# Experts in eleven passes instead of twelve, with a third expert of fixed place

## What is computed

```python
glog = hf @ w_rg + b_rg                       # 4 groups
gsel = argmax(glog);  gw = softmax(glog)[gsel]
elog = (hf @ w_re + b_re)[group gsel]         # 4 experts of that group
top_v, top_i = top_k(elog, 2)
wts  = softmax(top_v) * gw
act  = silu(hf @ w_gate[e]) * (hf @ w_up[e]) * comb[e]   # 1024 -> 256
out  = sum over experts of act @ w_down[e]               # 256 -> 1024
```

## Time and profile before

| | |
|---|---|
| time, median of 3 runs | 797.34 us (795.62 to 798.36) |
| span of the profiled execution | 795.5 us |
| median of the runs less that span | 1.84 us |
| PE busy | 762.2 us, 96% |
| DMA bytes | 136.50 MB, mean 172 GB/s |
| passes | 12 (12 gathers of rows, 12 stores) |

### The profile page before, as it was taken

One profiled execution on the slowest core, in us unless ns is written; L12 is line 12 of the kernel. 1 busy time (PEld: TensorE's weight loads), 2 busy tenths in 40 slices (PEclk: granted clock), 3 DMA queues, 4 the chain that ended last, 5 costly groups with the idle time before them and its releaser, 6 DMA issues.

```text
span 795.5 us, 12983 instructions
## 1 busy us (share of the span) xinstructions
PE 762.2 (96%) x5070; PEld 494.9 (62%) x5070; DVE 379.9 (48%) x850; ACT 204.9 (26%) x485; POOL 106.8 (13%) x160
## 2 busy tenths in 40 slices
PE   8999999999999999889999999999999999998995
PEld 5455588777778788555566775445556564654442
DVE  3269523997232323766624378434732212214865
ACT  3011213112223354654523200134111111123223
POOL 3000006000000311334500100011111101015002
PEclk9999999999999999999999999999999999999998
DMA  9640493841440499200030279003799999996002
GB/s 324 160 126 0 112 278 139 99 133 57 140 97 17 139 233 266 94 1 1 1 120 2 96 216 384 1 14 128 282 407 409 416 418 416 417 373 211 17 14 106
DMA packets 81287, 136.50 MB, mean 172 GB/s; under 512 B 33926, under 2 KB 57546, under 8 KB 77010
## 3 DMA queue, kind: packets, MB, share of 16 engines
q1 hardware_dynamic: 64700, 110.17, 41.7%
q0 software_dynamic: 3728, 13.38, 4.9%
q10 hardware_dynamic: 12798, 12.12, 4.6%
HBM read 116.55 MB, written 21.19 MB: 173 GB/s over the span
## 4 chain that ended last, share of the span: by engine, by line
PE 80%; DMA 8%; DVE 6%; issue 2%; ACT 2%; POOL 1%; DVEq 0%; SPq 0%; POOLq 0%; ACTq 0%
PE ps L1215 29%; PE ps L1300 10%; PE ps L1656 6%; PE ps L1904 5%; PE ps L1788 4%; PE ps L1222 3%; PE ps L1776 3%; DMA merged<-in_w_exp_down 3%; DMA w_slot<-in_w_exp_down 2%; PE ps L1441 2%; PE ps L1820 2%; PE ps L1491 2%; PE ps L1537 2%; PE ps L1518 2%; DMA wgu<-expert_rows,pos_i 1%
## 5 line engine op out<-in xcount | busy, mean ns | idle before, releaser
L1215 PE MATMUL ps<-w_slot,hT 128*128 128x396 f32 (+1 forms) x192 | 71.1, 529 | 0.6 <-DMA w_slot<-in_w_in 0.4
L1215 PE MATMUL ps<-hT,w_slot 128*128 128x288 f32 x256 | 63.1, 407 | 0.0
L1215 PEld LDWEIGHTS ps<-hT,w_slot 128*128 128x128 f32 x256 | 48.3, 190 | 13.9 <-issue 0.8
L1215 PEld LDWEIGHTS ps<-w_slot,hT 128*128 128x128 f32 x192 | 36.1, 190 | 32.5 <-issue 13.4
L2987 DVE SCALAR_TENSOR_TENSOR th<-th,ps 128x256 f32<-128x256 f32 x12 | 5.1, 421 | 103.2 <-ACT th L2248 103.2
L1788 PE MATMUL ps<-w_slot,hT 128*32 128x256 f32 x544 | 49.7, 380 | 0.0
L1300 PE MATMUL ps<-hT,w_slot 128*128 128x288 f32 x144 | 37.3, 407 | 0.0
L1215 PE MATMUL ps<-qg,w_slot 128*128 128x288 f32 x128 | 33.7, 408 | 0.0
L1788 PEld LDWEIGHTS ps<-w_slot,hT 128*32 128x32 f32 x544 | 26.3, 110 | 10.0 <-issue 2.3
L2728 DVE TENSOR_REDUCE nm_p<-ps 128x2 f32<-128x256 f32 (+3 forms) x32 | 25.0, 819 | 15.6 <-PE ps L1491 15.5
L1300 PEld LDWEIGHTS ps<-hT,w_slot 128*128 128x128 f32 x144 | 27.3, 190 | 7.6 <-issue 0.2
(11 more groups left out here) (508 smaller groups left out, 1416.5 us busy)
## 6 DMA issues: line engine op xcount, KB each, us to landing
merged<-in_w_exp_down SPq DMA_DIRECT2D x10, 1024.0 KB, 15.9
w_slot<-in_w_in SPq DMA_DIRECT2D x8, 1024.0 KB, 7.7
wgu<-in_w_exp_gate SPq DMA_DIRECT2D x8, 1024.0 KB, 12.1
wgu<-in_w_exp_up SPq DMA_DIRECT2D x8, 1024.0 KB, 14.1
w_slot<-in_w_exp_gate SPq DMA_DIRECT2D x8, 1024.0 KB
w_slot<-in_w_exp_up SPq DMA_DIRECT2D x8, 1024.0 KB
w_slot<-in_w_exp_down SPq DMA_DIRECT2D x6, 1024.0 KB
expert_rows<-onsaT ACTq DMA_DIRECT2D x12, 512.0 KB, 8.2
```

The lines of the kernel that those rows point to most:

```text
L1215: ins = pe.matmul(out, a, b, start=(n == 0), stop=(n == len(pairs) - 1))
```

## The change

There are 11 passes. The first one holds 96 rows of expert 0 and 32 of expert 1, the second the other 64 of expert 1 and a column of 64. Expert 2 is the third expert of fixed place and has the third pass to itself with 128 places. The other columns are 128, 128, four of 96 and seven of 64. The columns' order of loading is new, and so is the order on SP's queue. The gate and up weights of expert 2 are loaded as set 3 behind the second down load, before the router's order is known; set 2 is loaded behind the wait for the first gather as before. The first pass is now computed by `gate_up_of_two`, and the lists of rows and places are put together accordingly (`rows_of_passes`, the tables of GpSimd, the first list on VectorE).

```diff
-RANK_OF_COLUMN = [0, 1, 6, 2, 7, 8, 3, 9, 10, 4, 14, 5, 11, 12, 13, 15]
-COLUMNS_OF_PASS = [[0], [1, 12], [2, 12], [3], [4, 13], [5, 13], [6], [7, 14], [8, 14], [9], [10, 15], [11]]
+RANK_OF_COLUMN = [0, 1, 2, 5, 6, 3, 7, 8, 9, 10, 4, 11, 12, 13, 14, 15]
+UNITS_OF_PASS = [[0, 0, 0, 1], [1, 1, 11, 11], [2] * 4, [3, 3, 3, 12], [4, 4, 4, 12], [5] * 4, [6, 6, 6, 13], [7, 7, 7, 13],
+                 [8, 8, 14, 14], [9, 9, 15, 15], [10] * 4]
...
-LOADED = [0, 1, 12, 2, 3, 4, 13, 5, 6, 7, 14, 8, 9, 10, 15, 11]
+LOADED = [0, 1, 11, 2, 3, 12, 4, 5, 6, 13, 7, 8, 14, 9, 15, 10]
...
             load_down(1, 1)
+            load_gate_up(3, 2)
             sp.wait_ge(order_made, 1)
-            at_column = {0: 0, 1: 1}
+            at_column = {0: 0, 1: 1, 2: 2}
...
             sp.wait_ge(hg_ld[0], 16)
-            for l in range(2, NX):
-                read_column(l)
-                load_gate_up(l, expert(l))
+            read_column(2)
+            load_gate_up(2, expert(2))
             load_down(2, expert(2))
...
                 gate_up_weights(5)
+                gate_up_weights(6)
                 down_weights(3)
-                gate_up_weights(6)
                 gate_up_weights(7)
                 down_weights(4)
+                down_weights(5)
                 gate_up_weights(8)
-                down_weights(5)
                 down_weights(6)
                 gate_up_weights(9)
+                gate_up_weights(10)
                 down_weights(7)
-                gate_up_weights(10)
                 gate_up_weights(11)
                 down_weights(8)
+                down_weights(9)
                 gate_up_weights(12)
-                down_weights(9)
                 down_weights(10)
                 gate_up_weights(13)
+                gate_up_weights(14)
                 down_weights(11)
-                gate_up_weights(14)
                 gate_up_weights(15)
                 down_weights(12)
                 down_weights(13)
...
                 pe.matmul(out[:, 0:NPASS], ident[:], by_column[:, 0:NPASS], start=True, stop=True)
+                pe.matmul(out[96:P, 0:1], ident[:, 0:32], by_column[:, 1:2], start=True, stop=True)
                 for h in range(2):
-                    pe.matmul(out[96:P, 1 + h:8 + h:3], ident[:, 32 * h:32 * h + 32], by_column[:, 12:15], start=True, stop=True)
-                return pe.matmul(out[64:P, 10:11], ident[:, 0:64], by_column[:, 15:16], start=True, stop=True)
+                    pe.matmul(out[96:P, 3 + h:7 + h:3], ident[:, 32 * h:32 * h + 32], by_column[:, 12:14], start=True, stop=True)
+                pe.matmul(out[0:64, 1:2], ident[:, 32:96], by_column[:, 1:2], start=True, stop=True)
+                pe.matmul(out[64:P, 1:2], ident[:, 0:64], by_column[:, 11:12], start=True, stop=True)
+                return pe.matmul(out[64:P, 8:10], ident[:, 0:64], by_column[:, 14:16], start=True, stop=True)
...
-                gate_up(j, 0, 0, lambda: turn_rows(j, 1, 1, 0))
+                gate_up_of_two(j, 0, 0, lambda: turn_rows(j, 1, 1, 0))
...
-            tt(idx[:, 0:1], first_f[:, 0:1], o[:, NE:NE + 1], ALU.add).then_inc(first_made, 1)
+            tt(idx[0:96, 0:1], first_f[0:96, 0:1], o[0:96, NE:NE + 1], ALU.add)
+            tt(idx[96:P, 0:1], first_f[0:32, 1:2], o[0:32, NE + 1:NE + 2], ALU.add).then_inc(first_made, 1)
```

More of the change, by code:

```diff
@@ L61 @@
 MAXR = -(-ROWS // CAP)
-RANK_OF_COLUMN = [0, 1, 6, 2, 7, 8, 3, 9, 10, 4, 14, 5, 11, 12, 13, 15]
-COLUMNS_OF_PASS = [[0], [1, 12], [2, 12], [3], [4, 13], [5, 13], [6], [7, 14], [8, 14], [9], [10, 15], [11]]
-NPASS = len(COLUMNS_OF_PASS)
+RANK_OF_COLUMN = [0, 1, 2, 5, 6, 3, 7, 8, 9, 10, 4, 11, 12, 13, 14, 15]
+UNITS_OF_PASS = [[0, 0, 0, 1], [1, 1, 11, 11], [2] * 4, [3, 3, 3, 12], [4, 4, 4, 12], [5] * 4, [6, 6, 6, 13], [7, 7, 7, 13],
+                 [8, 8, 14, 14], [9, 9, 15, 15], [10] * 4]
+NPASS = len(UNITS_OF_PASS)
 OF_PARITY = [-(-NPASS // 2), NPASS // 2]
-LOADED = [0, 1, 12, 2, 3, 4, 13, 5, 6, 7, 14, 8, 9, 10, 15, 11]
-LAST_PASS = [max(n for n, columns in enumerate(COLUMNS_OF_PASS) if column in columns) for column in LOADED]
+LOADED = [0, 1, 11, 2, 3, 12, 4, 5, 6, 13, 7, 8, 14, 9, 15, 10]
+LAST_PASS = [max(n for n, columns in enumerate(UNITS_OF_PASS) if column in columns) for column in LOADED]
 NX = 4
@@ L73, in unit_loads @@
 def unit_loads(n):
-    loads = [LOADED.index(column) for column in COLUMNS_OF_PASS[n]]
-    own = 2 if COLUMNS_OF_PASS[n][-1] == NE - 1 else 3
-    return [loads[0]] * own + [loads[-1]] * (4 - own)
+    return [LOADED.index(column) for column in UNITS_OF_PASS[n]]
 def down_before(l):
@@ L1101, in row_of @@
                 pool.iota(out, [[step, out.shape[-1]]], base=first, channel_multiplier=0, allow_small_or_imprecise_dtypes=True)
[L1102 to L1106, removed]
+            pool.memset(base_at[:, 0:1], 0.0)
+            pool.memset(base_at[:, 1:2], 96.0)
+            row_of(base_at[:, 2:NPASS], 2 * CAP, CAP)
+            pool.memset(base_at[:, 11:12], float(CAP + 64))
+            row_of(base_at[:, 12:14], 3 * CAP + 96, 3 * CAP)
+            row_of(base_at[:, 14:16], 8 * CAP + 64, CAP)
+            for at, cap in ((slice(0, 2), 96), (slice(2, 3), 128), (slice(3, 5), 96), (slice(5, 6), 128), (slice(6, 8), 96),
+                            (slice(8, 10), 64), (slice(10, 11), 128), (slice(11, 16), 64)):
                 pool.memset(cap_at[:, at], float(cap))
-            for at, split in ((slice(0, 12), 0), (slice(12, 15), 1), (slice(15, 16), 0)):
+            for at, split in ((slice(0, 12), 0), (slice(12, 14), 1), (slice(14, 16), 0)):
                 pool.memset(split_at[:, at], float(split))
-            for e in range(2):
+            for e in range(3):
                 pool.memset(first_at[:, e:e + 1], float(2 ** (21 - e)))
-            row_of(first_at[:, 2:NE], NE - 3, -1)
-            for at in (slice(0, 2), slice(2, 3), slice(3, 4), slice(4, 6), slice(6, 7), slice(7, 9), slice(9, 10), slice(10, 11),
-                       slice(11, 12), slice(12, 15), slice(15, 16)):
+            row_of(first_at[:, 3:NE], NE - 4, -1)
+            for at in (slice(0, 3), slice(3, 5), slice(5, 6), slice(6, 10), slice(10, 11), slice(11, 16)):
                 row_of(rank_of[:, at], RANK_OF_COLUMN[at.start], 1)
@@ L1777, in gate_up, with gate_up_of_two @@
                 ins.then_inc(g_done, 1)
-            def gate_up_of_two(j, n, u):
+            def gate_up_of_two(j, n, u, between=None):
                 weights_there(j, n)
@@ L1783, in gate_up_of_two @@
                     for k in range(KD):
+                        if w and k == 4 and between:
+                            between()
                         if w == 0 and k % 4 == 0:
@@ L1824, in of_two @@
             def of_two(n):
-                return len(COLUMNS_OF_PASS[n]) == 2
+                return len(set(UNITS_OF_PASS[n])) == 2
             def turn_rows_of_tile0(j):
```

## The result

The changed kernel takes 802.12 us (median of 13 runs, 798.76 to 805.63), the kernel before 798.08 us in as many (795.08 to 801.81). Forecast were 798.1 us and no change; the result lies just inside the upper end of the range (802.5), where the case "the clock falls in the new waits" had put it (801.5).

The account below looks back on a forecast made before the run. The prediction took TensorE and DMA transfers as joint bounds of the expert stage; a 4.4 us gain, lost at the last loads, left +0.6 plus 0.2 us, so 797.34 became 798.1 us, range 793.3 to 802.5.

Parts of the forecast that it names:

- the clock falls in the new waits: Rival: TensorE at half clock behind new waits of about 4 us, two falls of 1.7 us, 801.5 us; chance 0.32.
- Before the passes: Ahead of the expert passes: small extra work 0.2 us; first gather slowed by early loads, first pass about 1.6 us later.
- TensorE and transfers: Expert passes: one pass (11.72 us) less, but transfers bound; ninth down product ends at 693.2 against 697.65, gain 4.4 us.
- Where it goes: Last three loads, behind one wait on a dry queue beside store and gathers: last down product starts +0.6 us later.
- Behind the last down product: Store, tile 1's gathers and embedding part after the last down product: nothing changes, all follow at the old distance.
- these 2 us: Tile 0 may be done 2 us sooner, its gathers ending before 718; not counted because tile 1's rows come last.
- the sum: Whole kernel: +0.6 us at the last down product plus 0.2 us for what precedes, span 795.5 to 796.3 us.
- The rivals: Alternatives to the forecast: volume comes out 0.15, all of the pass 0.03, clock falls 0.32, a second round 0.01.
- How the numbers follow: Chances for the whole kernel: tail takes the gain back 0.49; faster 0.19, same 0.48, slower 0.33.
- stand alone between long full stretches: Argument against the clock falling in TensorE's new waits, unlike the attention part's many short gaps; that case had chance 0.32.

Follow-up runs that it names:

- e3: Changed kernel with the third expert's gate and up weights loaded behind the second set again, not early; ratio 1.0024 to the kernel before.
- e9: Changed kernel with tile 0's two gathers held until the last down weights have landed; one run, 800.38 us.
- e6: Changed kernel with useless products in three waits (3 before tenth gate and up, 2 before ninth down, 6 before last down); ratio 1.0008 to the kernel before.
- e10: Changed kernel with 6 useless products in one wait alone, ahead of the last down product; ratio 1.0033 to the kernel before.
- e4: Changed kernel with the second set of weights issued ahead of the wait for the first gather; ratio 1.0064 to the kernel before.
- e11: Changed kernel with useless products in two waits (3 before tenth gate and up, 2 before ninth down), none before last down; ratio 1.0065 to the kernel before.
- e12: Changed kernel with embedding-gate weights ahead of the last two down loads and expert 2's early load behind the experts' order; ratio 0.9979 to the kernel before.

## Why the prediction was wrong

*Before the passes.* The gather took 8.71 us (8.4 taken) and the first turn came 2.0 us later behind its issue (1.6 forecast). What I left out: the third set landed only at 581.80, so the second pass's gate and up began 19.7 us behind the gather's issue, where it had begun at 16.9 (577.76 less 560.89). e3 shows that most of it was taken up again by the ninth pass.

*TensorE and transfers.* TensorE was no longer the bound, and the waits stood where the forecast had them: ahead of the tenth gate and up (3.15 us), the ninth down (1.09) and the last down (5.50); one ahead of the ninth gate and up (1.39) came on top. The ninth pass's rows were stored 2.8 us sooner than the third from the end of before; 4.4 were forecast. The 2.10 MB of the early load had been counted as 5.1 us out of the full stretch, well above the price of the late start; e3, without the early load, stored these rows at the same 134.6 (one execution of each), so by then it had brought nothing.

*Where it goes.* Right in its mechanism: three loads out together behind the ninth down product, on a dry queue, beside a store and two gathers, whose share e9 measured once. From that product's end to the last down it took 18.3 us (714.57 less 696.23) against 17.5 forecast (710.7 less 693.2). With the smaller gain before it, the last down product began 3.0 us later than in before where +0.6 had been forecast: a term mis-sized by 2.4 us.

*Behind the last down product.* I had everything follow at the old distance, 10.1 us. Without a fall it is 7.9 to 8.0 (e6, e10), since in before tile 0 had waited for its gathers (2.02 us ahead of the line at 720.20). I had named these 2 us and set them aside for tile 1, which did not hold them back: the rest behind the turn is 75.0 us in e6. This second error of 2.1 us about cancels the first: with the clock held the change costs +0.6 us (1.0008), and the sum had said +0.8. That agreement is partly luck.

*The step that failed* is in "The rivals" and "How the numbers follow": the falls of the clock were given 0.32, on the ground that the waits "stand alone between long full stretches". Here that protected nothing. In after the clock was 0.57 from 682 to 686, behind the wait of 3.15 us, and 0.50 from 716 to 720, behind that of 5.50, and e6 shows that holding it in all three waits takes 4.0 of the 4.6 us away. The rival's working was only partly right. It wanted two falls on the path at 1.7 us each; e10 shows the last on the path, at 2.8 us in after's profile (10.8 less 8.0) and 2.0 by the ratios, and behind the wait ahead of the ninth down the clock stayed at 1.00 (692 to 696). The other half of the 4.0 us is not assigned, and neither is the overlap of all this with the 2.7 us that e3 gained without touching the waits.

## What to carry to other kernels

A new wait of TensorE can have two prices, its length and the slower clock of the work behind it; where that work leads straight to the next stage, put the second into the sum. When a gain is given back at a stage's last loads, look first at what stands in the queue ahead of the last one needed: here 2.1 MB that nobody needed yet cost more than the change had gained, and moving them ahead of or behind the last two down loads made the change pay. A short fill of useless products, cut to the length of the wait, is a cheap test for the clock; price one of them first.

## What the runs showed of the hardware

The same fall has different lengths. From the start of the last down product the clock stayed at 0.50 for 5.5 us in after (to 720.1), 5.7 in e4, 3.1 in e11 and 2.9 in e3. From there to the turn of tile 0 it took 10.8, 10.9, 9.5 and 9.6 us, against 7.9 without a fall: the excess is about half of the time at 0.50. Nor does a wait's length alone tell whether a fall follows: ahead of the ninth down product a wait of 2.33 us in e10 was followed by 1.00 (692 to 696), one of 2.27 us in e12 by 0.57. And code that the change doesn't touch had the clock at 0.50 from 321 to 324 us in some executions and at 1.00 in others. The Trainium skill, "TensorE: Matmul & The Clock Gate", Part 1, says of a kernel's start that the number of matmuls run before the clock rises differs from run to run of the same kernel. The rows here agree in kind only, since they are single executions of four kernels and lie behind waits. By them, a price read from one profile can be off by more than 1 us (10.9 less 9.5).
